# First norm by feature-wise weights, reordered window attention, split projections and five moved waits in a chain of two transformer blocks

## The reference

```python
def rmsnorm(x, g):
    xf = x.astype(f32)
    y = xf * lax.rsqrt(jnp.mean(xf * xf, axis=-1, keepdims=True) + EPS)
    return (y * g.astype(f32)).astype(x.dtype)

def swiglu(x, w_gate, w_up, w_down):
    return (jax.nn.silu(x @ w_gate) * (x @ w_up)) @ w_down
...
    x = x + 0.5 * swiglu(rmsnorm(x, norm_ffn1), ffn1_gate, ffn1_up, ffn1_down)
```

## Time and profile before

| | |
|---|---|
| median of three runs | 1165.45 us (1164.42 to 1166.35) |
| the profiled execution | 1165.28 us, of it span 1163.6 us |
| busy in the span | TensorE 98%, VectorE 74%, ScalarE 56%, GpSimd 5% |
| read from memory | 261.31 MB, 226 GB/s on average |

### The profile page before, as it was taken

The page is one execution under the profiler, slowest core; times in us unless marked ns, Lnnn a source line. Parts: engine busy times, 40 slices in busy tenths (PEclk is TensorE's granted clock), DMA queues, the critical chain, the costliest instruction groups (busy, mean ns, idle before and its releaser), DMA issues.

```text
span 1163.6 us, 16120 instructions
## 1 busy us (share of the span) xinstructions
PE 1140.6 (98%) x6230; PEld 961.1 (83%) x6230; DVE 866.5 (74%) x1385; ACT 651.5 (56%) x1084; POOL 61.0 (5%) x77
## 2 busy tenths in 40 slices
PE   6999999999999999999998999999999999999998
PEld 5888888888889888888885778888888887888887
DVE  6788976656667779999688778888777758677654
ACT  5554654556665465555477555555556865555551
POOL 1000000000001000500032000000020001000000
PEclk9999999999999999999999999999999999999999
DMA  8786984755445489999542167888737534677641
GB/s 330 269 289 238 341 289 145 281 187 182 145 167 177 155 321 329 350 336 336 183 149 90 57 253 259 320 294 306 277 138 275 194 109 148 224 242 249 239 147 37
DMA packets 42380, 263.45 MB, mean 226 GB/s; under 512 B 7360, under 2 KB 7744, under 8 KB 12480
## 3 DMA queue, kind: packets, MB, share of 16 engines
q1 hardware_dynamic: 42304, 262.42, 63.3%
HBM read 261.31 MB, written 1.10 MB: 226 GB/s over the span
## 4 chain that ended last, share of the span: by engine, by line
PE 87%; DVE 6%; issue 3%; ACT 2%; POOL 1%; DMA 1%; SPq 0%; POOLq 0%; DVEq 0%; ACTq 0%
PE ps L351 85%; DVE wl L1024 2%; PE ps L520 1%; PE ps L937 1%; PE ps L698 1%; DMA raw<-in_stream 1%; DVE xn L1136 1%; POOL res L2035 0%; DVE xn L1073 0%; POOL small L2029 0%; DVE arena L1462 0%; ACT wh L1634 0%; DVE x L1059 0%; ACT arena L1657 0%; ACT arena L1887 0%
## 5 line engine op out<-in xcount | busy, mean ns | idle before, releaser
L1024 DVE TENSOR_TENSOR wl<-raw,wh 128x1024 fp32r<-128x1024 f32 x374 | 450.3, 1224 | 20.9 <-ACT wh L1634 20.2
L1634 ACT ACTIVATE wh<-raw 128x1024 fp32r<-128x1024 f32 x374 | 388.0, 1051 | 50.4 <-PE ps L351 28.6
L351 PE MATMUL ps<-x,wh 128*128 128x512 f32 x1568 | 393.3, 393 | 0.0
L351 PEld LDWEIGHTS ps<-x,wh 128*128 128x128 f32 x1568 | 285.3, 188 | 56.5 <-issue 2.0
L351 PEld LDWEIGHTS ps<-x,wl 128*128 128x128 f32 x1568 | 213.8, 190 | 15.4
L351 PE MATMUL ps<-x,wl 128*128 128x256 f32 x1568 | 218.5, 282 | 0.0
L351 PE MATMUL ps<-wh,x 128*128 128x512 f32 (+1 forms) x600 | 185.1, 385 | 1.6 <-DVE x L1059 1.5
L351 PE MATMUL ps<-wh,hh 128*128 128x512 f32 x404 | 160.0, 396 | 0.0
L351 PE MATMUL ps<-wl,hh 128*128 128x512 f32 x404 | 158.0, 391 | 0.0
L351 PE MATMUL ps<-wh,hl 128*128 128x512 f32 x404 | 157.3, 389 | 0.0
L351 PEld LDWEIGHTS ps<-wh,x 128*128 128x128 f32 x600 | 111.5, 190 | 24.3 <-issue 2.7
(11 more groups left out here) (182 smaller groups left out, 851.6 us busy)
## 6 DMA issues: line engine op xcount, KB each, us to landing
raw<-in_stream SPq DMA_DIRECT2D x233, 1024.0 KB, 5.1
arena<-vectors SPq DMA_DIRECT2D x12, 512.0 KB, 6.3
arena<-in_tables SPq DMA_DIRECT2D x7, 576.0 KB, 6.2
raw<-in_stream SPq DMA_DIRECT2D x4, 512.0 KB, 8.4
gain_sb<-in_gains SPq DMA_DIRECT2D x3, 512.0 KB, 8.5
res<-in_x SPq DMA_DIRECT2D x4, 256.0 KB, 5.3
gain_sb<-in_c SPq DMA_DIRECT2D x2, 512.0 KB, 7.0
out_dram<-res SPq DMA_DIRECT2D x3, 256.0 KB, 2.0
```

Source lines behind the costliest of these rows:

```text
L351: return e.matmul(o, a, b, start=start, stop=stop)
L1024: e.tensor_tensor(WL[:, n % NW, :], src, WH[:, n % NW, :].bitcast(F32), ALU.subtract).then_inc(*w_lo.tick(n))
L1634: e.activation(WH[:, m % NW, :], src, ACT.Copy).then_inc(*w_hi.tick(m))
```

## The change

- First norm: the gain is no longer broadcast over the rows. Rows are multiplied by 32 and the power (`first_rows`) and transposed into four banks, two feature tiles each (`first_move`); the gain, now one column for each feature tile, is a scale per partition in the copies (`first_high`, `first_low`). The loads are put in another order, the second piece of x is issued by ScalarE, and the load of c no longer waits for the first norm. 28 transposes of the identity stand ahead of TensorE's first work.
- Mixer: projection (qa, 1) moves ahead of the first pair, the rotation starts at another bank, and the last pair's values move ahead of (gb, 7).
- Sliding: `turn_q` stands after the values, `turned_heads` of tile 1's first half one iteration later, `weighted` after the minimum; the weight splits of iterations 6 to 12 move to 8 to 13 (VectorE) and 8 to 11 (ScalarE). The first four units of `wo_a` for t = 1 run unit by unit.
- Boundaries 4 and 6: weight splits stand at other places. Stick: k3's combination of pair 0 stands ahead of the subtraction for sl.

```diff
-M_FILL = {0: (("qa", 1), ("ka", 1), ("qa", 3)), 1: (("ka", 3), ("qa", 5), ("ka", 5))}
+M_AHEAD = [(x + "a", m) for m in (0, 2, 4) for x in "qk"] + [("qa", 1)]
+M_FILL = {0: (("ka", 1), ("qa", 3)), 1: (("ka", 3), ("qa", 5), ("ka", 5))}
...
-        for c in range(2):
-            e.dma_start(RES[0][c], halves(io["x"][0:P, :])[c]).then_inc(*x_in[c].tick())
-        i = GAINS.index("norm_ffn1")
-        first = halves(io["gains"][i:i + 1, :])
-        e.dma_start(GAIN[0][0], first[0].partition_broadcast(P)).then_inc(*half_gain_in.tick())
-        e.dma_start(GAIN[0][1], first[1].partition_broadcast(P)).then_inc(*gain_in[0].tick("norm_ffn1"))
+        e.dma_start(RES[0][0], halves(io["x"][0:P, :])[0]).then_inc(*x_in[0].tick())
         load_unit(0)
+        e.dma_start(first_gain, io["first_gain"]).then_inc(*first_gain_in.tick())
+        for i in range(1, 3):
+            load_unit(i)
         for c in range(2):
             e.dma_start(RES[1][c], halves(io["x"][P:2 * P, :])[c]).then_inc(*x_in[2 + c].tick())
-        for i in range(1, 2 * FIRST):
-            load_unit(i)
+        load_unit(3)
...
             if g == 7:
-                sp.wait_ge(*vec.of("out", 0, 1, 1))
                 e.dma_start(cond, io["c"].partition_broadcast(P)).then_inc(*c_in.tick(0))
...
+        def first_move(t, turn):
+            for j in range(4):
+                b = next(turn)
+                claim(b)
+                place["first", t, j] = b
+                pe.wait_ge(*vec.of("out", 0, t, j // 2))
+                for i in range(2):
+                    at = P * (2 * (j % 2) + i)
+                    z = e.transpose(bank(b, P, P * i), XN[t][j // 2][:, at:at + P], ident[:])
...
-            turn = itertools.cycle([5, 6, 7])
+            turn = itertools.cycle([7, 5, 6])
...
-                for fill in M_FILL[k]:
+                projection(*M_FILL[k][0])
+                if k == len(M_PAIRS) + 1:
+                    pair_values(k - 2)
+                for fill in M_FILL[k][1:]:
                     projection(*fill)
-                if k > 1:
+                if 1 < k < len(M_PAIRS) + 1:
                     pair_values(k - 2)
...
-                if i in (1, 7, 11):
-                    turn_q(*{1: (0, 1, 7), 7: (1, 0, 0), 11: (1, 1, 7)}[i])
                 if 2 <= i < 18:
                     p_tiles(i - 2)
...
                 if i > 2:
                     values(i - 3)
+                if i in (1, 7, 11):
+                    turn_q(*{1: (0, 1, 7), 7: (1, 0, 0), 11: (1, 1, 7)}[i])
...
-            for ks in (range(4), range(4, KT)):
+            for k in range(4):
                 for c in range(2):
-                    for k in ks:
-                        if (k, c) == (6, 1):
-                            move(4, 0, itertools.cycle([4, 5]))
-                        outward(k, 1, c)
+                    outward(k, 1, c)
+            for c in range(2):
+                for k in range(4, KT):
+                    if (k, c) == (6, 1):
+                        move(4, 0, itertools.cycle([4, 5]))
+                    outward(k, 1, c)
...
-        move(0, 0, turn)
+        for _ in range(28):
+            e.transpose(bank(7, P), ident[:], ident[:])
...
+        def first_rows(t, c):
+            dv.wait_ge(*x_in[2 * t + c].of())
+            dv.wait_ge(*pooled.of("power", 0, t))
+            e.tensor_scalar(XN[t][c], RES[t][c], rstd[t][:, 0:1], 32.0, ALU.mult, ALU.mult).then_inc(*vec.tick(("out", 0, t, c)))
+        def first_low(t, j):
+            dv.wait_ge(*first_gain_in.of())
+            dv.wait_ge(*x_hi.of("first", t, j))
+            for k in range(2 * j, 2 * j + 2):
+                cut = lambda x: x[:, k, P * t:P * t + P]
+                i = e.scalar_tensor_tensor(cut(XL), bank(place["first", t, j], P, P * (k % 2)), first_gain[:, k:k + 1],
+                                           cut(XH).bitcast(F32), ALU.mult, ALU.subtract)
...
+            lows = (1, 2, 3, 8, 10, 11, 12, 13)
             for i in range(19):
-                if i in (7, 11, 15):
-                    weighted(i // 4 - 1)
...
+                if i in lows:
+                    low_to(n + lows.index(i))
...
-                if i in (5, 9):
-                    turned_heads(1, 2 * i - 10, 8, bank(2 + i // 8), i == 5)
-                if i in (1, 2, 3, 6, 8, 10, 11, 12):
-                    low_to(n + (1, 2, 3, 6, 8, 10, 11, 12).index(i))
+                if i == 6:
+                    turned_heads(1, 0, 8, bank(2), True)
+                if i == 9:
+                    turned_heads(1, 8, 8, bank(3), False)
...
             y_low(3)
+            low_to(n + 1)
             mean_square(4, 0)
             normalised(4, 0)
-            low_to(n + 4)
+            low_to(n + 3)
...
+            low_to(n + 4)
             mean_square(4, 1)
-            low_to(n + 5)
             normalised(4, 1)
...
+                if between:
+                    combined(*between)
                 dv.wait_ge(*x_hi.of("sp", p))
                 e.tensor_tensor(sl, ksp[p % 2], sh.bitcast(F32), ALU.subtract).then_inc(*x_lo.tick(("sp", p)))
...
-            at(n, n - TAIL + NW)
-            boundary(6, "wo_b", n)
+            low_to(n + 1)
+            residual(6, 0, 0, "wo_b")
+            low_to(n + 2)
+            gained(6, 0, 0)
...
+            normalised(6, 0)
+            low_to(n + 3)
+            residual(6, 1, 0, "wo_b")
...
+            normalised(6, 1, n + 4)
...
         mean_square(0, 0)
         for c in range(2):
-            gained(0, 0, c)
-        normalised(0, 0)
+            first_rows(0, c)
         low_to(0)
-        x_low(0, 0)
-        low_to(1)
-        for c in range(2):
-            gained(0, 1, c)
+        for j in range(2):
+            first_low(0, j)
         low_to(2)
         mean_square(0, 1)
+        for c in range(2):
+            first_rows(1, c)
         low_to(3)
-        normalised(0, 1)
+        for j in range(2, 4):
+            first_low(0, j)
...
-                if i in (0, 2, 6, 8, 9, 10):
-                    high_to(n + 2 + (0, 2, 6, 8, 9, 10).index(i))
+                if i in (0, 2, 8, 9, 10, 11):
+                    high_to(n + 2 + (0, 2, 8, 9, 10, 11).index(i))
...
+            n = N["tm", "wo_a", KT - 1]
+            high_to(n + 1)
             square(4, 0, 1)
-            n = N["tm", "wo_a", KT - 1]
-            high_to(n + 4)
+            high_to(n + 5)
             x_high(4, 0)
...
+        e.dma_start(RES[0][1], halves(io["x"][0:P, :])[1]).then_inc(*x_in[1].tick())
         e.preload_act_table_set("silu_and_others")
         square(0, 0, 0)
         square(0, 0, 1)
         high_to(0)
-        x_high(0, 0)
-        high_to(1)
+        for j in range(2):
+            first_high(0, j)
+        high_to(2)
         square(0, 1, 0)
         square(0, 1, 1)
+        high_to(3)
+        for j in range(2, 4):
+            first_high(0, j)
```

More of the change, by code:

```diff
@@ L196, in program @@
     cond = gain_sb[:, 0, :]
+    first_gain = col(KT)
     mhalf = col(16)
@@ L640, in projection @@
                 evicted[b] = [vec.of(name, m)]
-            for m in (0, 2, 4):
-                projection("qa", m)
-                projection("ka", m)
+            for name, m in M_AHEAD:
+                projection(name, m)
             def pair_values(j):
@@ L1083, in gained @@
                 slot = GAIN_SLOT[GAIN_FOR[q]]
[L1084 to L1088, removed]
+                dv.wait_ge(*gain_in[slot].of(GAIN_FOR[q]))
+                dv.wait_ge(*vec.of("sum", q, t, c))
                 e.scalar_tensor_tensor(x, r, 32.0, GAIN[slot][c], ALU.mult, ALU.mult).then_inc(*vec.tick(("gained", q, t, c)))
@@ L1177, in ffn @@
             low_to(n + TAIL - 1)
-            x_low(q, 1)
+            if q:
+                x_low(q, 1)
+            else:
+                for j in range(4):
+                    first_low(1, j)
             for k in range(TAIL, KT):
@@ L1315, in combined @@
                     *vec.tick((name, m)))
-            for m in (0, 2, 4):
-                for name in ("qa", "ka"):
-                    at(N["fm", name, m])
-                    combined(name, m)
+            for name, m in M_AHEAD:
+                at(N["fm", name, m])
+                combined(name, m)
             def y_low(tile_):
@@ L1355, in mixer @@
                     combined(name, m)
-                j = k - 2
-                if j >= 0 and M_PAIRS[j][2]:
+                if 0 <= j < len(M_PAIRS) - 1 and M_PAIRS[j][2]:
                     kind, hp, t = M_PAIRS[j]
@@ L1536, in masked, with terms @@
                     *vec.tick(("masked", p)))
-            def terms(p):
+            def terms(p, between=None):
                 dv.wait_ge(*acted.of("log", p))
@@ L1568, in stick @@
                 at(N["fm", "k3", p + 1] if p < KT - 1 else N["tm", "wo_b", 1])
-                terms(p)
-                if p < KT - 1:
+                terms(p, None if p else ("k3", 1))
+                if 0 < p < KT - 1:
                     combined("k3", p + 1)
@@ L1646, in x_high, with first_high @@
```

(19 more changed lines are left out.)

36 lines of the change are left out of this document (27 added, 9 removed).

## The result

The changed kernel takes 1156.87 us (median of 4 runs, 1156.76 to 1156.99) against 1165.75 us before (4 runs, 1164.42 to 1166.35): ratio 0.9925, 95% interval 0.9908 to 0.9943. The forecast was 1155.3: 8.9 us were gained of the 10.1 that it added up. The profiled span fell from 1163.6 to 1155.0 us, by 8.5.

A forecast was written before the change was run, and what follows sets the result against it. TensorE, busy 98%, was taken to bound the kernel, so only its waits or slow stretches could yield time. Terms 4.0 + 0.4 + 0.7 + 2.9 + 1.2 + 0.9 = 10.1 gave 1155.3 us, range 1153 to 1157.

The forecast's parts named there:

- three rivals: Whole kernel: warm-up without effect 1156.5 (chance 0.17), sliding's waits returning elsewhere 1157.2 (0.17), start bound by transfers 1157.2 (0.10).
- The start: First norm and first weight units: unit 4 of row tile 0 done at 18.9 instead of 22.9, gaining 4.0 us.
- The warm-up rival: Start: transposes warm nothing, clock stays 1.2 GHz for two units, 1.2 us lost, total 1156.5; chance 0.17.
- First pair: Mixer's first pair: a projection placed in between hides the scores' wait for a combination (L1314), gaining 0.4 us.
- k3: Stick breaking: scores 1 no longer wait for k3's combination (L1558), gaining 0.9 us (0.4 to 1.1).
- Sliding: Sliding attention: four waits totalling 3.2 us mostly go, gaining 2.9 us (1.0 to 3.6).
- the first 0.6: Sliding, iteration 6: scores wait for the subtraction of maxima behind VectorE's head turn; they come 0.6 us earlier.
- the 1.3 of scores 8: Sliding: wait L1865 at the end of head turn, transposes, copy, scores 8; moves up, 0.3 us left there.
- the second 0.6: Sliding: the other L1462 wait, a low half ahead of the scores' subtraction; moving five low halves later removes it.
- The rival that the waits come back elsewhere: Sliding: VectorE sets the pace, moved work only changes which wait is last; gain 1.0, total 1157.2; chance 0.17.
- The mixer's end: Mixer's end: a projection hides the 0.9 wait (L1324), 0.2 kept as a new wait, gaining 0.7 us (0.3 to 0.9).
- Boundaries 4 and 6: Waits before the transposes of normalised rows (L1136 twice, 1.5 together): gain 1.2 us for both (0.5 to 1.7).

The follow-up runs named there:

- no_warm_up: The changed kernel without the 28 transposes of the identity ahead of TensorE's first work: 1157.18 us, +0.31 to the changed kernel.
- mixer_banks: The changed kernel with the mixer's upward products going through the banks in the order 4, 6, 7, 5: 1156.71 us, -0.16 to the changed kernel.
- mixer_tuned: The changed kernel with upward banks 4, 6, 7, 5 and two low halves moved behind VectorE's multiplication: 1156.35 us, -0.52 to the changed kernel.
- start_alone: The kernel before with all changes of the start, warm-up transposes included, and none of the others: 1161.24 us, ratio 0.9964 to before.

## Why the prediction was right, point by point

**The whole.** 1156.87 is 1.6 above the forecast and nearer to the times of three rivals (1156.5, and 1157.2 twice). The total alone does not choose between them; the timelines do.

**The start: 4.0 predicted, 4.1 to 4.2 measured.** Most of its chain is in the trace to a few tenths: unit 0 at 6.50 (6.5), warm-up done at 7.33 (7.4), VectorE's chain from 7.60 (7.6) to 17.47, the end of unit 4's low half (17.8). One step was wrong without harm: the rows are scaled by 7.67, not by 6.7, because x landed 1.0 later than before, for which the prediction had no term; no run shows why. That just fits behind unit 0's high half, done at 7.56. That VectorE hands over the units is shown by no_warm_up: products slower by 0.2 each, until 13, cost 0.3 in all.

**The warm-up rival fell on its mechanism, and its price was too high.** It had the clock low for two units and 1.2 us lost. The transposes did raise the clock, and even without them only 0.3 are lost, since TensorE has waits of 0.51 and 0.99 for low halves in that stretch to fill. The Trainium skill ("TensorE: Matmul & The Clock Gate", Part 4: PE-mode transpose) states that a transpose in that mode doesn't count as busy in the same way. These runs show otherwise for the float32 transposes of this kernel: x's first eight take 1.06 behind the 28 and 1.94 without them. The measurement decides; the trace calls them MATMUL and doesn't tell whether they run in that mode.

**First pair 0.4, k3 0.9: measured 0.65 and 0.89** (put back: 0.66 and 1.05 less 0.1). The waits went and nothing took their place. Of the pair only the size was off: its term was the listed wait.

**Sliding 2.9: measured 3.0 to 3.4, but for the wrong reason in part.** The prediction gave the turn's order the first 0.6 and the 1.3 of scores 8, and the low halves only the second 0.6. The runs give the turn 0.6 and the low halves 2.4. The step that failed is the chain "head turn, transposes, copy, scores 8": what held the copy was the low half of iteration 6, ahead of the subtraction of scores 7, whose exponentials stand ahead of the copy on ScalarE. The sum came right by luck, because the change moved both. The rival that the waits come back elsewhere fell: in sliding none is listed at over 0.2. The 3.4 has another 0.5 in it, from the order of the first outward products; it shows at boundary 4, and the prediction had no term for it.

**The mixer's end: 0.7 predicted, -0.2 measured.** "I keep 0.2 as a new wait" named the right bank and the right releaser (L1351, listed at 0.2), but this was not all that is late next. The step that failed is that an earlier start of the upward products is kept. VectorE's multiplications, which empty their banks, start with the sigmoid, behind ScalarE's last copy and a table load of 1.28; the change doesn't bring these forward (they come 0.2 later). TensorE started 0.9 earlier only to wait at two banks. mixer_banks shows it: with the first of these waits gone another of 0.35 comes at 358.99, on the multiplications. mixer_tuned, which brings some of the multiplications forward, gets 0.43 of the gain.

**Boundaries 4 and 6: 1.2 predicted, 0.1 measured** (0.36 and -0.26). The waits for normalised rows went, 0.88 and 0.61 by the timelines. The prediction took 0.3 off for what a low half would show behind the normalisation; 0.51 came back in boundary 4 (671.38), 0.36 in boundary 6 (973.49), and boundary 6 has a second wait (970.49) of 0.57. The step that failed there is that the other low half "moves into VectorE's wait for GpSimd's sum" free of charge: the sum took 0.91 longer. That this is what makes the low half at 970.49 late is read from the order of VectorE's work; no run has the new order with a fast sum. The Trainium skill ("SBUF — State Buffer", Who interferes with whom) states that a VectorE instruction with two SBUF inputs contends with a GpSimd instruction that reads SBUF, and that one with at most one SBUF input, outside VectorE's two-port modes, does not. The trace agrees: beside the low half (raw and wh) the sum takes 2.20 and the power 1.47 instead of 0.55; beside the subtraction from PSUM (ps and x, 964.79) the sum keeps its 1.29.

**The sum.** 10.1 predicted, 8.5 in the profiles. The mixer's end (0.9) and the boundaries (1.1 to 1.2) are the miss; the start, the pair and sliding gave 0.3 to 0.5 more than their terms. So the total is near because errors of both signs met in it.

## What to carry to other kernels

Follow a step's gain to the next instruction that needs the same engine: TensorE that starts earlier gains only if the engine that empties its banks starts earlier too. Before work is moved into an engine's idle time, look at what ends that time: if it is GpSimd and the work reads two SBUF operands on VectorE, the wait grows. Match the same instructions in two timelines to see what a step brought, since the listed waits (0.4 for a stop that costs 0.66) understate it; and put back the halves of a step separately, since a right sum can hide wrong parts.

## What the hardware showed unexpectedly

28 transposes of a 128x128 float32 identity, and nothing else, were enough for TensorE's fast level: in start_alone they ended after 4.61 us, in the changed kernel after 5.70. In all twelve kernels that have them x's eight transposes took 1.04 to 1.08 behind them, and 1.94 in the one that has not. GpSimd's power of a 128x1 column takes 0.55 alone and 1.47 beside a VectorE subtraction of two SBUF operands of 1024.
